# A decoder layer on one core: modulation and first projections by chunk, the second gate in the value stage, norm 1 by token tile

## The reference

```python
ada = jax.nn.silu(c) @ w_ada[l] + b_ada[l]
sh1, sc1, gt1, sh2, sc2, gt2 = jnp.split(ada[:, None, :], 6, axis=-1)
h = x * (1.0 + sc1) + sh1
proj = h @ w_in[l]
qa, ka, va, hq, hf, hi, hg, ga, gb = jnp.split(proj, split_at, axis=-1)
ya = moba_attention(qa.reshape(mh), ka.reshape(mh), va.reshape(mh))
yb = hgrn2(hq, hf, hi, hg, lb_all[l], hgrn_norm_g[l])
mixed = (jax.nn.sigmoid(ga) * (ya @ w_branch_a[l])
         + jax.nn.sigmoid(gb) * (yb @ w_branch_b[l]))
x = layer_norm(DEEPNORM_ALPHA * x + gt1 * (mixed @ w_out[l]), ln1_g[l], ln1_b[l])
h2 = x * (1.0 + sc2) + sh2
y = peer(h2, peer_wq[l], peer_subkeys[l], peer_u[l], peer_v[l])
x = layer_norm(DEEPNORM_ALPHA * x + gt2 * y, ln2_g[l], ln2_b[l])
```

## Time and profile before

| | us |
|---|---|
| median of 3 runs | 1103.84 |
| lowest and highest run | 1102.63, 1103.85 |
| the profiled execution | 1103.95 |
| its span | 1102.2 |
| TensorE busy (94%) | 1034.2 |
| VectorE busy (66%) | 732.0 |
| ScalarE busy (45%) | 496.4 |
| GpSimd busy (35%) | 388.4 |

### The profile page before, as it was taken

The page is one execution under the profiler, slowest core; times in us unless marked ns, Lnnn a source line. Parts: engine busy times, 40 slices in busy tenths (PEclk is TensorE's granted clock), DMA queues, the critical chain, the costliest instruction groups (busy, mean ns, idle before and its releaser), DMA issues.

```text
span 1102.2 us, 18076 instructions
## 1 busy us (share of the span) xinstructions
PE 1034.2 (94%) x7078; PEld 960.4 (87%) x7078; DVE 732.0 (66%) x1551; ACT 496.4 (45%) x746; POOL 388.4 (35%) x185
## 2 busy tenths in 40 slices
PE   1599999798799999999999999999999999999996
PEld 1599988697799999999999999998888888888885
DVE  6687998786469805955666677776555665555556
ACT  1346454642344445454434433435554544455552
POOL 3023432200077877886666666640001000000002
PEclk9999999898799999999999999999999999999998
DMA  8788774554345555554444444436557765556651
GB/s 283 279 285 314 252 255 158 174 172 141 108 152 177 177 183 172 180 185 154 147 139 136 141 145 137 141 111 228 190 192 243 278 197 192 194 192 193 193 195 52
DMA packets 58347, 204.91 MB, mean 186 GB/s; under 512 B 6675, under 2 KB 8723, under 8 KB 58259
## 3 DMA queue, kind: packets, MB, share of 16 engines
q1 hardware_dynamic: 56806, 198.51, 54.7%
q0 software_dynamic: 1456, 5.25, 1.3%
HBM read 201.63 MB, written 2.10 MB: 185 GB/s over the span
## 4 chain that ended last, share of the span: by engine, by line
PE 88%; DVE 7%; DMA 2%; issue 2%; ACT 1%; POOL 0%; SPq 0%; DVEq 0%; ACTq 0%
PE px L918 31%; PE pw L664 15%; PE pw L665 15%; PE pw L666 15%; PE px L890 5%; DVE acc L974 2%; DMA ada<-in_w_ada 2%; PE pv L664 1%; PE pv L665 1%; PE pv L666 1%; DVE w_lo L962 1%; PE px L856 1%; ACT w_hi L438 0%; DMA acc<-in_b_ada 0%; DVE xT L996 0%
## 5 line engine op out<-in xcount | busy, mean ns | idle before, releaser
L438 ACT ACTIVATE w_hi<-raw 128x1024 fp32r<-128x1024 f32 x324 | 342.0, 1057 | 411.2 <-PE px L918 159.5
L360 POOL TENSOR_TENSOR w_lo<-raw,w_hi 128x1024 fp32r<-128x1024 f32 x148 | 362.5, 2450 | 262.7 <-ACT w_hi L438 179.8
L664 PE MATMUL pw<-a_hi,w_hi 128*128 128x256 f32 x1376 | 400.1, 291 | 18.6 <-DVE a_lo L1005 12.5
L665 PE MATMUL pw<-a_lo,w_hi 128*128 128x256 f32 x1376 | 391.9, 285 | 0.0
L666 PE MATMUL pw<-a_hi,w_lo 128*128 128x256 f32 x1376 | 391.9, 285 | 0.0
L962 DVE TENSOR_TENSOR w_lo<-raw,w_hi 128x1024 fp32r<-128x1024 f32 x176 | 215.1, 1224 | 179.4 <-ACT w_hi L438 174.2
L664 PEld LDWEIGHTS pw<-a_hi,w_hi 128*128 128x128 f32 x1376 | 266.7, 194 | 21.2 <-issue 14.6
L665 PEld LDWEIGHTS pw<-a_lo,w_hi 128*128 128x128 f32 x1376 | 267.0, 194 | 0.1
L666 PEld LDWEIGHTS pw<-a_hi,w_lo 128*128 128x128 f32 x1376 | 266.4, 194 | 0.0
L918 PE MATMUL px<-w_hi,ws_hi 128*128 128x512 f32 x512 | 159.0, 389 | 0.9 <-DVE ws_lo L1313 0.9
L918 PE MATMUL px<-w_lo,ws_hi 128*128 128x512 f32 x512 | 159.0, 389 | 0.0
(11 more groups left out here) (290 smaller groups left out, 932.7 us busy)
## 6 DMA issues: line engine op xcount, KB each, us to landing
raw<-in_u SPq DMA_DIRECT2D x128, 512.0 KB, 3.6
raw<-in_v SPq DMA_DIRECT2D x128, 512.0 KB, 4.6
raw<-in_ws SPq DMA_DIRECT2D x68, 512.0 KB, 4.7
ada<-in_w_ada SPq DMA_DIRECT2D x48, 512.0 KB, 5.8
xT<-in_xT SPq DMA_DIRECT2D x1, 1024.0 KB, 9.0
x_nat<-in_x SPq DMA_DIRECT2D x1, 1024.0 KB, 5.0
x_spill<-x POOLq DMA_DIRECT2D x1, 1024.0 KB, 6.5
x_b<-x_spill POOLq DMA_DIRECT2D x1, 1024.0 KB, 8.2
```

The lines of the kernel that those rows point to most:

```text
L360: nc.gpsimd.tensor_tensor(w_lo[:, m % RING], raw[:, m % RING], w_hi[:, m % RING].bitcast(F32), ALU.subtract) \
L438: return nc.scalar.activation(out, in_, ACT.Copy, **kw)
L664: nc.tensor.matmul(out, lh, rh, start=start and x == 0, stop=False)
L665: nc.tensor.matmul(out, lh, rl, start=False, stop=False)
```

## The change

- **Start.** Blocks 0 to 5 (HF, HQ, HI; `FIRST` = 6) no longer come from the ring. The input dimension is cut in eight chunks of 128. Chunk c has its own column slice of w_ada (`ada1`, 128x2048, 1 MB), a slice of x, and a slice of the six blocks' weights (`w1`, 128x1536, 768 KB), each in three slots. VectorE sums the slice (`sum_part`), TensorE makes four one-column sums (`mod1`), ScalarE adds the bias and writes h and its rounded part, VectorE the rest (`h_lo`), and TensorE adds the chunk's part of all six blocks, in six PSUM banks (`first_block`). The sums of chunk c + 1 stand behind block 4 of chunk c.
- **Order.** HGATE moves from block 6 to block 12. HGRN, attention and everything with a block number between them move two blocks earlier. The natural-order blocks use one bank, a half for each token tile, in place of two.
- **Branches.** ya and yb are split into their own place (`y_hi`, `y_lo`), yb at block 21, ya at block 22.
- **Gate 2.** Its 8 tiles of w_ada leave the front (24 tiles stay, `ada_at` from block 6 on). They are loaded and summed on VectorE in the value stage, one every four pieces from v piece 70 on, and TensorE makes the broadcast row in two PSUM banks after v piece 112 with four matmuls of 512 columns (in place of L813 before). The trip through HBM goes.
- **Norm 1.** w_out's last block runs tile by tile (`rows_block`: tile 0 with both pieces, then tile 1; one bank each). VectorE does statistics tile by tile; ScalarE normalises tile 0, VectorE tile 1; transposes and h2 go by tile and half, and the pieces of block 31 are split behind the norm.

```diff
-HF, HQ, HI, HGATE, QA, KA, VA, GA, GB = 0, 2, 4, 6, 8, 10, 12, 14, 18
+HF, HQ, HI, QA, KA, VA, HGATE, GA, GB = 0, 2, 4, 6, 8, 10, 12, 14, 18
...
-UP = 2 * NA
+FIRST = 6
...
+CHUNK_SLOTS = 3
+GT2_ROW, GT2_LOAD, GT2_SUM, GT2_ADD = 60, 70, 72, 112
...
+        y_hi = sb("y_hi", AR + 3072, [KC, T], F32R)
+        y_lo = sb("y_lo", AR + 5120, [KC, T], F32R)
...
+            for c in range(KC):
+                load_ada1(c)
+                if c < 3:
+                    load_x(c)
+                load_raw1(c)
...
+                r = m - VP
+                if GT2_LOAD <= r < GT2_LOAD + 4 * KC and (r - GT2_LOAD) % 4 == 0:
...
+                    sp.dma_start(ada2[k % 2][:, :], w_ada_d[k * P:(k + 1) * P, 3 * D:4 * D]).then_inc(ada2_landed[k % 2], 16)
...
+            for c in range(KC):
+                act.wait_ge(x_chunk_landed[0 if c == 0 else 1 if c < 4 else 2], 16)
+                act.wait_ge(mod1_done, c + 1)
+                for s in range(2 * c, 2 * c + 2):
+                    last = nc.scalar.activation(mod1[:, s:s + 1], px[0][:, s:s + 1], ACT.Identity, bias=b_cols[:, s:s + 1])
+                last.then_inc(mod1_copied, 1)
+                act.wait_ge(mod1_copied, c + 1)
+                for out in (a_hi, xT):
+                    last = nc.scalar.activation(out[:, c], xT[:, c], ACT.Identity, scale=mod1[:, 2 * c + 1:2 * c + 2],
+                                                bias=mod1[:, 2 * c:2 * c + 1])
+                last.then_inc(h_hi_ready, 1)
+                if c + 1 < KC:
+                    split_hi1(c + 1)
...
                 if HGATE <= e < HGATE + 2:
                     r = e - HGATE
-                    for t, src in enumerate((pw[s], pv[s])):
-                        last = nc.scalar.activation(sgh[:, t, r * 256:(r + 1) * 256], src[:, 0:256], ACT.Sigmoid)
-                    last.then_inc(sig_done, 1)
+                    nc.scalar.activation(sgh[:, :, r * 256:(r + 1) * 256], pw[s][:, :].rearrange("p (a n) -> p a n", a=TT),
+                                         ACT.Sigmoid).then_inc(sig_done, 1)
...
+                if b == 21:
                     for t, src in enumerate((pv[1], px[3])):
                         act.wait_ge(ybT_done, t + 1)
-                        last = copy(a_hi[:, 4:8, t * P:(t + 1) * P], src[:, :].rearrange("p (h t) -> p h t", h=HG))
+                        last = copy(y_hi[:, 4:8, t * P:(t + 1) * P], src[:, :].rearrange("p (h t) -> p h t", h=HG))
                     last.then_inc(act_hi, 1)
+                if b == 22:
+                    act.wait_ge(ya_copied, HEADS // 2)
+                    copy(y_hi[:, 0:4], yaT[:, :, :]).then_inc(act_hi, 1)
...
+                    root(0)
+                    act.wait_ge(shift1_ready, 1)
+                    for half in range(2):
+                        q = slice(half * 512, (half + 1) * 512)
+                        nc.scalar.activation(x1[:, 0, q], x1[:, 0, q], ACT.Identity, scale=rstd[:, 0:1], bias=shift1[:, :]) \
+                            .then_inc(xn_ready[0], 1)
...
+                    h2_columns(0, (0, 1))
+                    root(1)
+                    h2_columns(0, (2, 3)).then_inc(h2f_act_ready, 1)
+                    act.wait_ge(h2f_act_ready, 1)
+                    h2_hi(0, 0)
+                    act.wait_ge(x1T_done, 2)
+                    h2_columns(0, range(4, 8)).then_inc(h2f_act_ready, 1)
+                    act.wait_ge(h2f_act_ready, 2)
+                    h2_hi(0, 1)
+                    act.wait_ge(h2f_ready, 1)
+                    h2_hi(1, 0)
+                    act.wait_ge(x1T_done, 4)
+                    h2_columns(1, range(4, 8)).then_inc(h2f_act_ready, 1)
+                    act.wait_ge(h2f_act_ready, 3)
+                    h2_hi(1, 1)
+                    split_block(b)
...
+            def rows_block(b, x_hi, x_lo):
                 for t, bk in enumerate((pw[b % 2], pv[b % 2])):
                     q = slice(t * P, (t + 1) * P)
-                    last = three(bk[:, 0:256],
-                                 [(x_hi[:, 4 * h + k, q], x_lo[:, 4 * h + k, q], hi[:, k], lo[:, k])
-                                  for k in range(KC // 2)], start=h == 0, stop=h == 1)
-                last.then_inc(piece_used, 1)
+                    for h in range(2):
+                        hi, lo = (w.rearrange("p (k c) -> p k c", k=KC // 2) for w in weights(2 * (b - FIRST) + h))
+                        last = three(bk[:, 0:256], [(x_hi[:, 4 * h + k, q], x_lo[:, 4 * h + k, q], hi[:, k], lo[:, k])
+                                                    for k in range(KC // 2)], start=h == 0, stop=h == 1)
+                        if t:
+                            last.then_inc(piece_used, 1)
+                    if t == 0:
+                        last.then_inc(tile0_done, 1)
...
+            def mod1(c):
+                pe.wait_ge(part_ready, c + 1)
+                for s in range(2):
+                    for i in range(2):
+                        last = nc.tensor.matmul(px[0][:, 2 * c + s:2 * c + s + 1], part[c % 2][:, i, s * P:(s + 1) * P],
+                                                ones_col[:, :], start=i == 0, stop=i == 1)
+                last.then_inc(mod1_done, 1)
...
+            def first_block(b, c):
+                hi, lo = (w[c % 2][:, 256 * b:256 * (b + 1)] for w in (hi1, lo1))
+                for s in range(2):
+                    q = slice(s * P, (s + 1) * P)
+                    pair = (a_hi[:, c, q], a_lo[:, c, q], hi, lo) if b in NATURAL else (hi[:, q], lo[:, q], a_hi[:, c], a_lo[:, c])
+                    last = three(p1[b][:, s * T:(s + 1) * T], [pair], start=c == 0 and s == 0, stop=c == KC - 1 and s == 1)
...
-            for c in range(2 * KC):
-                if c % KC == 0:
-                    pe.wait_ge(ada_done, c + KC)
-                last = nc.tensor.matmul(px[0][:, c:c + 1], acc[:, 0, c * P:(c + 1) * P], ones_col[:, :],
-                                        start=True, stop=True)
...
+            mod1(0)
+            for c in range(KC):
+                pe.wait_ge(lo1_ready, c + 1)
+                pe.wait_ge(h_lo_ready, c + 1)
+                for b in range(FIRST):
+                    last = first_block(b, c)
+                    if b == 4 and c + 1 < KC:
+                        mod1(c + 1)
+                if c < KC - 1:
+                    last.then_inc(chunk_used, 1)
...
-                if b == WOUT + 1:
-                    pe.wait_ge(gt1_ready, 1)
-                    for half in range(2):
-                        last = nc.tensor.matmul(px[half][0:1, :], ones_col[:, :],
-                                                acc[:, 0, ADA_W + half * 512:ADA_W + (half + 1) * 512], start=True, stop=True)
-                    last.then_inc(gt2_done, 1)
...
+                if v == GT2_ADD:
+                    pe.wait_ge(gt2_summed, KC)
+                    for half in range(2):
+                        for s in range(2):
+                            last = nc.tensor.matmul(pw[half][:, :], ones_pp[:, :], gt2_acc[s][:, half * 512:(half + 1) * 512],
+                                                    start=s == 0, stop=s == 1)
...
+                    def tile(t):
+                        dve.wait_ge(tile0_done if t == 0 else piece_used, 1 if t == 0 else used(e))
+                        ins = v.tensor_tensor(x1[:, t, q], (pw, pv)[t][s][:, 0:256], gt1[:, q], ALU.mult)
...
+                        link(v.scalar_tensor_tensor(x1[:, t, q], x_nat[:, t, q], ALPHA, x1[:, t, q], ALU.mult, ALU.add))
+                        link(v.bn_stats(bn[:, (4 * t + 3) * 6:(4 * t + 4) * 6], x1[:, t, q]))
+                        link(v.bn_aggr(mv[:, 2 * t:2 * t + 2], bn[:, 24 * t:24 * t + 24]))
+                        v.tensor_scalar(std[:, t:t + 1], mv[:, 2 * t + 1:2 * t + 2], LN_EPS, None, ALU.add).then_inc(var_ready, 1)
...
+                    tile(0)
+                    inverse(0)
+                    v.scalar_tensor_tensor(shift1[:, :], mv[:, 0:1], -1.0, rstd[:, 0:1], ALU.mult, ALU.mult).then_inc(shift1_ready, 1)
+                    tile(1)
+                    inverse(1)
...
+                    dve.wait_ge(mod2_ln_ready, 1)
+                    h2_lo(0, 0)
+                    dve.wait_ge(x1T_done, 3)
+                    for k in range(4):
+                        ins = v.tensor_scalar(h2f[:, k, P:T], px[2][:, k * P:(k + 1) * P],
+                                              mod2[:, KC + k:KC + k + 1], mod2[:, k:k + 1], ALU.mult, ALU.add)
+                    ins.then_inc(h2f_ready, 1)
+                    h2_lo(0, 1)
+                    h2_lo(1, 0)
+                    h2_lo(1, 1)
+                    split_lo(2 * (b - FIRST))
+                    split_lo(2 * (b - FIRST) + 1)
...
                 split_w(r)
+                if GT2_SUM <= r < GT2_SUM + 4 * KC and (r - GT2_SUM) % 4 == 0:
+                    k = (r - GT2_SUM) // 4
...
+                        ins = v.scalar_tensor_tensor(a[:, :], ada2[k % 2][:, :], sc_col[:, k:k + 1], a[:, :], ALU.mult, ALU.add)
```

(1 more changed line is left out.)

532 lines of the change are left out of this document (308 added, 224 removed).

## The result

The changed kernel takes **1085.99 us** (median of 4 runs, 1084.18 to 1086.25) against 1103.84 (1102.63 to 1105.77) for the kernel before: ratio 0.9833, 95% interval 0.9815 to 0.9851: faster, clear of noise, though by less than 2%. The forecast was 1082.2, in a range of 1074 to 1093. Run again beside other kernels it took 1083.81 us (5 runs, 1083.44 to 1085.85) against 1103.3, ratio 0.9832 (0.9809 to 0.9855); the text calls this the rerun.

A forecast was written before the change was run, and what follows sets the result against it. TensorE was taken as the bound from about 311 us on, with pauses only before. Terms -11.7 + 1.0 - 6.9 - 1.7 - 5.9 + 3.5 = -21.7 gave 1082.25 from 1103.95; predicted 1082.2, range 1074 to 1093.

The forecast's parts named there:

- Start: Blocks 0 to 5, run chunk by chunk: they end at 69.3 us instead of 81.03, -11.7 us.
- the term of the first chunk: Kernel start: loads, VectorE's eight operations, column sums and hand-overs let TensorE start its first projection matmul at 14.8 us.
- Middle: Blocks 6 to 21: the HGRN gate between the heads adds four table loads, mostly hidden; +1.0 us, bounds 0 to 6.6.
- branch wait: Before the branch blocks: TensorE's pause goes, -6.9 us (5.0 of pause, 1.9 of clock).
- Covered: Block 23: both gates' sigmoids, about 5 us of ScalarE, are late next but hidden until the first branch block is done.
- The gt2 row's 1.7 us: After block 27: the gt2 row, 1.88 us, goes from there, for -1.7 us.
- Norm 1: Between w_out's end and WQ: WQ starts 9.2 us after that end instead of 15.1, -5.9 us.
- value stage: Value stage: gate 2's four matmuls of 128x512 come onto TensorE's path, +3.5 us, bounds 1.8 and 3.8.
- A: Rival, start: the clock falls once in each chunk and recovers, 12.6 us more, 1095; chance 7%.
- B: Rival, chunks 0 to 7: whole chunk stage at the lower clock, 26.6 us later than forecast, 1109; chance 3%.
- C: Rival, middle: between the heads, table loads and a later f starve splits, 4 to 7 us more, 1088; chance 11%.
- D: Rival, better overlap: chunk cycle 6.3 us, WQ at 8 us after w_out's end, table loads hidden, 1076; chance 16%.

The follow-up runs named there:

- late clearing: Against the changed kernel, GpSimd clears the sums' buffer only after VectorE has made its first part; 1081.65 us, ratio 0.9809.
- the kernel with the longer waits: Against the changed kernel, VectorE makes each chunk's low half three times over, so TensorE waits longer for every chunk; 1093.21 us (one run).

## Why the prediction was right, and where it was short

**Start, -9.85 for -11.7.** The loop was right: 6.86 us for 6.9, with a clock at 1.00. By its own steps, the term of the first chunk was mis-sized: 16.79 us for 14.8. It counted VectorE's eight operations at 0.42 us and looked only at VectorE's inputs, not at what GpSimd does at that time, although held a scaling of 2.46 us of the same kind. The late clearing gives 14.57 us and shows it.

**Middle and branch wait, -4.46 and -1.73 for -4.0 and -1.9.** The pause went, and the matmuls behind it are 0.12 us apart at once. The +1.0 for the table loads was 0; without them nothing moves. That the middle came within 0.5 us of its sum is in part luck: without the pause of 4.95 us it is 0.5 us longer than before, of which 0.3 are a longer wait for w_lo (1.5 for 1.2) and 0.2 stay open. The Trainium skill, "ScalarE: Activation LUTs", "What ACT_TABLE_LOAD costs", counts a drain beside each load; here the activation starts 0.02 us after a load of 1.28 us, so by the page the term, +4, would have been further off.

**"Covered" was wrong.** The forecast said that the sigmoids at block 23 are the next thing to be late, and hidden. They made VectorE 2.1 us late at the end of the branch stage, and w_out's first block waited 1.4 us. It took the pause as gain and did not ask who else had used it: before, ScalarE's table load and a part of its sigmoids lay in the pause, and they ended 2.6 us behind the first branch matmul (214.34 for 211.79), now 6.8 (204.32 for 197.48). The gt2 row's 1.7 us went into that wait, so w_out gave 0.42 us. Moving one sigmoid removes the wait.

**Norm 1 and value stage, -6.12 and +3.4 for -5.9 and +3.5.** Each comes out alone: +6.3 us when norm 1's code is undone, -3.4 us when the value stage's product is left out. For norm 1 the sum of its two parts is shown, not each.

**Rivals.** A: no fall at waits of 1.42 us; at 3.06 us it comes, and VectorE hides it. B is out. C: no more wait at the heads than before. D's shorter cycle came only with another place of the folding (6.11 and 5.20 us), which the change does not have.
The Trainium skill, "TensorE: Matmul & The Clock Gate", on HAM oscillation, describes such a fall in every turn of a loop of short bursts, with longer waits than the changed kernel has. The changed kernel shows none, and the kernel with the longer waits shows one in every second turn.

**The last 2 us.** The three later of the first four runs stood 1.6 to 2.1 us above the profiled one, and the spread of single runs goes with the granted clock: 1080.2 and 1085.7 us of one kernel at 0.992 and 0.986, 1071.5 and 1075.7 of another at 0.994 and 0.987. Short low stretches come and go or change their length: the one in the middle (six profiles of thirteen) and the one in w_out (3.4 or 6.8 us) are worth 1.5 us each. For the first four runs of the changed kernel the clock reads 0.989 each time, so for those it remains open.

## What to carry to other kernels

Where a chain runs through several engines in each turn, place the smallest link of it first: moving four one-column matmuls from block 4 to block 0, with the sums they need made a turn ahead, brought 8.5 us by the profile and 11.2 by the medians, where the whole new start had brought 9.85. When a pause goes, list every engine that caught up in it, and check the first order of business behind it. And read what the other engines do beside the first operations of a critical chain; here a clearing that nobody was waiting for added 2 us to them. A run that puts a piece of code back shows the worth of all that the piece holds, and not of the part in its name.
